# A decoder step with 32 experts: passes of 32 tokens on four column tiles in place of 64 on two

## What is computed

```
top_v, top_i = lax.top_k(h @ r_w + r_b, 4);  top_w = softmax(top_v)      # 4 of 32 experts per token
for e in range(32):
    gu   = h @ w_gu[e] + b_gu[e]                                         # 1024 -> 2048
    gate = min(gu[:, :1024], 7);  up = clip(gu[:, 1024:], -7, 7)
    act  = (up + 1) * gate * sigmoid(1.702 * gate)
    out += combine[:, e] * (act @ w_dn[e] + b_dn[e])                     # 1024 -> 1024
```

```
25 34 47 33 31 60 29 48 24 29 36 25 46 47 42 48 28 36 30 73 44 39 57 19 21 37 29 40 35 79 71 38
```

## Time and profile before

| what | value |
|---|---|
| runs, us | 1500.16, 1504.97, 1509.39; median 1504.97 |
| span of the profiled execution, us | 1507.8 (it has no time of its own beside the span; 2.8 above the median, within the runs) |
| PE busy | 1460.0 us, 97% |
| DVE, ACT busy | 441.6 us, 29%; 197.3 us, 13% |
| moved | 470.78 MB, mean 312 GB/s |
| first expert product, last one | 461.1 us, 1485.7 us |

### The profile page before, as it was taken

The page is one execution under the profiler, slowest core; times in us unless marked ns, Lnnn a source line. Parts: engine busy times, 40 slices in busy tenths (PEclk is TensorE's granted clock), DMA queues, the critical chain, the costliest instruction groups (busy, mean ns, idle before and its releaser), DMA issues.

```text
span 1507.8 us, 18412 instructions
## 1 busy us (share of the span) xinstructions
PE 1460.0 (97%) x6676; PEld 654.1 (43%) x6677; DVE 441.6 (29%) x1096; ACT 197.3 (13%) x334; POOL 21.3 (1%) x35
## 2 busy tenths in 40 slices
PE   5999999999979999999999999999999999999996
PEld 2655566666754333333333333333333333333333
DVE  3133332323373223222322322232232223223226
ACT  2120013000021101111110110111011111111102
POOL 0000000000000000000000000000000000000000
PEclk9999999878998999999999999999999999999998
DMA  9877351104325999999999999997999999996380
GB/s 390 314 286 294 113 181 63 74 12 135 131 112 223 375 417 418 418 417 417 419 418 417 417 419 419 416 417 316 360 418 419 416 418 419 419 416 261 129 332 35
DMA packets 87366, 470.78 MB, mean 312 GB/s; under 512 B 7936, under 2 KB 7952, under 8 KB 51280
## 3 DMA queue, kind: packets, MB, share of 16 engines
q1 hardware_dynamic: 84416, 460.68, 75.5%
q0 software_dynamic: 2352, 7.75, 1.9%
q10 hardware_dynamic: 576, 2.04, 0.3%
HBM read 465.59 MB, written 4.85 MB: 312 GB/s over the span
## 4 chain that ended last, share of the span: by engine, by line
PE 84%; DMA 8%; SPq 5%; DVE 2%; issue 1%; ACT 0%; DVEq 0%
PE bank L866 25%; PE bank L900 14%; PE bank L581 12%; DMA ring<-in_exp_w_gu 7%; PE bank L797 6%; PE bank L778 6%; SPq L434 5%; PE bank L713 3%; PE bank L728 2%; PE bank L579 2%; PE bank L884 1%; PE bank L891 1%; PE bank L664 1%; PE bank L785 1%; PE bank L644 1%; DMA ring<-in_ada_w 1%
## 5 line engine op out<-in xcount | busy, mean ns | idle before, releaser
L866 PE MATMUL bank<-ring,big 128*64 128x512 f32 x2240 | 490.4, 593 | 6.9 <-DMA ring<-in_exp_w_gu 6.9
L866 PEld LDWEIGHTS bank<-ring,big 128*64 128x64 f32 x2240 | 158.2, 137 | 317.6 <-issue 286.2
L900 PE MATMUL bank<-ring,big 128*64 128x512 f32 x1120 | 257.7, 602 | 0.0
L1516 DVE TENSOR_SCALAR big<-bank 128x512 f32<-128x512 f32 x35 | 24.2, 692 | 685.5 <-PE bank L866 685.5
L581 PE MATMUL bank<-hT,ring 128*128 128x320 f32 (+1 forms) x592 | 177.3, 461 | 4.2 <-DVE hT L1161 3.1
L581 PEld LDWEIGHTS bank<-hT,ring 128*128 128x128 f32 (+1 forms) x592 | 117.5, 201 | 69.4 <-issue 27.8
L900 PEld LDWEIGHTS bank<-ring,big 128*64 128x64 f32 x1120 | 74.6, 137 | 129.7 <-issue 127.3
L1505 DVE TENSOR_TENSOR gates<-gates,bank 128x320 f32<-128x320 f32 x272 | 114.2, 481 | 44.5 <-PE bank L797 44.5
L797 PE MATMUL bank<-big 64*128 64x320 f32 x560 | 114.1, 457 | 2.3 <-DVE xT L1559 1.6
L778 PE MATMUL bank<-vtok,big 128*64 128x512 f32 x432 | 100.8, 602 | 0.3 <-DVE big L1446 0.3
L797 PEld LDWEIGHTS bank<-big 64*128 64x128 f32 x560 | 64.0, 185 | 51.5 <-issue 34.9
(11 more groups left out here) (273 smaller groups left out, 846.7 us busy)
## 6 DMA issues: line engine op xcount, KB each, us to landing
ring<-in_exp_w_gu SPq DMA_DIRECT2D x256, 1024.0 KB, 18.1
ring<-in_exp_w_dn SPq DMA_DIRECT2D x128, 1024.0 KB, 16.1
ring<-in_ada_w SPq DMA_DIRECT2D x24, 1024.0 KB, 20.6
ring<-in_w_in SPq DMA_DIRECT2D x20, 1024.0 KB, 9.7
ring<-in_w_out SPq DMA_DIRECT2D x4, 1024.0 KB, 8.5
ring<-in_w_in SPq DMA_DIRECT2D x4, 528.0 KB, 10.4
S<-in_state_hgrn POOLq DMA_DIRECT2D x4, 512.0 KB, 7.5
out_hgrn_sample<-S POOLq DMA_DIRECT2D x4, 512.0 KB, 3.8
```

The lines of the kernel that those rows point to most:

```text
L866: ins = mm(banks[1 + m][64 * h:64 * h + 64, :], h2g[:, half(k)], ring[:, item_slot(k), c:c + 512], start=False, stop=(k == DC - 1))
L900: ins = mm(banks[4][64 * h:64 * h + 64, :], actT[:, half(k)], pair(item_slot(DC + k // 2))[:, k % 2, h * 512:(h + 1) * 512], start=(k == 0 ...
```

## The change

CAP becomes 32. An item's 32 tokens are the stationary operand in four column tiles of 32: tile g holds columns 256g to 256g+255 of each half of the output, so one instruction covers 256 gate and 256 up columns (`gu`, one bank), or 256 columns of `w_dn`'s output. All [128 x 512] buffers of an item become [128 x 256]. The scatter reads 32 rows per feature block, in four row tiles.

All items run in one loop. PE's is now a loop over pairs of experts with an inner loop over the items of each (the table holds the first item of each expert, and item tables are built before item 0). The output biases go through the scatter of item 0, from `dng`, into a `yacc` that is set to zero first. SP's rule stays: buffer s of an expert waits for the last item of the expert before. `NAHEAD` is 0, so the branch that would give some buffers a second home (`late`) is not taken; `late` only gathers tiles of the first stages at one address.

```diff
-CAP = 64
+CAP = 32
+NAHEAD = 0
+GRP = P // CAP
+HALF = D // GRP
...
-        SCATTER = [3, 5, 4, 6, 7, 0, 6, 7]
+        SCATTER = [4, 5, 6, 7, 4, 5, 6, 7]
+        FEATURES = [2 * (n % GRP) + n // GRP for n in range(DC)]
...  SP
-            def expert(e, i):
+            def expert(e, odd, last1, last2):
...
                     elif s == 7:
-                        sp.wait_ge(up_ready, i + 1)
+                        sp.wait_ge(gu_ready, used + 1)
                     elif s == 11:
-                        sp.wait_ge(dn_ready, i + 1)
+                        sp.wait_ge(dn_ready, used + 1)
                     else:
-                        sp.wait_ge(slot_used, i * 10 + (USED0 + (s if s < 7 else s - 1) + 1))
+                        sp.wait_ge(slot_used, used * 10 + (USED0 + (s if s < 7 else s - 1) + 1))
...
-            with sp.Fori(1, E) as e:
-                expert(e, sp.value_load(itemtab[0:1, ds(e + NI, 1)], min_val=0, max_val=NI - 1))
+            expert(1, True, last_item(0), None)
+            with sp.Fori(1, E // 2) as pairs:
+                e = pairs * 2
+                expert(e, False, last_item(e - 1), last_item(e - 2))
+                expert(e + 1, True, last_item(e), last_item(e - 1))
...  PE, one item
-                for m in range(2):
-                    for h in range(2):
-                        mm(banks[1 + m][64 * h:64 * h + 64, :], bsel[0:96, :], bgu[0:96, m * D + h * 512:m * D + (h + 1) * 512],
-                           start=True, stop=False)
+                for g in range(GRP):
+                    mm(out[part(g), :, :], bsel[0:96, :], bias[0:96, :, columns(g)], start=True, stop=False,
+                       tile_position=(0, CAP * g))
                 for k in range(DC):
...
+                    w = item_buffer(k, odd).rearrange("p (m c) -> p m c", m=2)
+                    for g in range(GRP):
+                        last = mm(out[part(g), :, :], h2g[:, chunk(k)], w[:, :, columns(g)], start=False, stop=(k == DC - 1),
+                                  tile_position=(0, CAP * g))
+                    last.then_inc(gu_ready if k == DC - 1 else slot_used, 1)
                 gather(i + 1)
+                pe.wait_ge(dn_copied, i + 1)
+                pe.wait_ge(selw_copied, i + 1)
+                pe.wait_ge(summed, i * 8 + 1)
+                scatter(i, range(GRP))
                 pe.wait_ge(act_ready, i + 1)
...              two transposes of the activation
+                flip_gathered(i + 1)
+                scatter(i, range(GRP, 2 * GRP))
                 pe.wait_ge(act_copied, i + 1)
                 for k in range(DC):
...
+                    for g in range(GRP):
+                        last = mm(banks[2][part(g), HALF:2 * HALF], actT[:, chunk(k)],
+                                  pair(item_slot(DC + k // 2))[:, k % 2, columns(g)],
+                                  start=(k == 0), stop=(k == DC - 1), tile_position=(0, CAP * g))
+                    if k % 2:
+                        last.then_inc(dn_ready if k == DC - 1 else slot_used, 1)
+                flip_weights(i + 1)
...  scatter
+                    x, g = n // GRP, n % GRP
+                    if n >= GRP:
+                        pe.wait_ge(summed, i * 8 + (n - GRP + 2))
+                    mm(banks[SCATTER[n]][:, 0:T], dng[part(g), x * P:(x + 1) * P], SelWT[part(g), :],
+                       start=True, stop=True, tile_position=(CAP * g, 0)).then_inc(scattered, 1)
...  PE's loops
+            with pe.Fori(0, E // 2) as pairs:
+                e = pairs * 2
+                n0, n1, n2 = first_item(e), first_item(e + 1), first_item(e + 2)
+                with pe.Fori(n0, n1) as i:
+                    item(i, pairs, False)
+                with pe.Fori(n1, n2) as i:
+                    item(i, pairs, True)
...  DVE, before item 0
+            nc.vector.memset(yacc[:, :, :], 0.0).then_inc(summed, 1)
```

More of the change, by code:

```diff
@@ L41 @@
 NI = E + MAXEXTRA + 1
+NTHR = -(-T // CAP)
 EPS = 1e-6
@@ L256, in build @@
         SelWT = take(T)
-        gtok = take(512)
-        h2g = take(DC * CAP)
-        gbuf, ubuf, sbuf_, actb, actT, dng = (take(512) for _ in range(6))
+        gtok, h2g = take(HALF), take(HALF)
+        gbuf, ubuf, sbuf_, actb, actT, dng = (take(HALF) for _ in range(6))
+        off[0] = 2 * HT + 2048
         bgu = take(1024).bitcast(BF16)
-        bsel = take(32).bitcast(BF16)
+        bdn = take(HALF)
+        bsel = take(CAP // 2).bitcast(BF16)
         posI = take(3 * NI).rearrange("p (a i) -> p a i", a=3)
@@ L264, in build @@
         OHI = take(NI)
+        ohi_from = take(NI)
         yacc = gates
@@ L279, in build @@
         ngt = rtake(1)
[L280 to L283, removed]
+        over = rtake(NTHR, 1)
+        nitems, bounds = rtake(1, 1), rtake(2, 1)
         posT = small[0:E, 0:T]
-        combT = small[0:E, T:2 * T]
-        logT = combT
-        thrrep = rtake(P, 1)
+        logT = small[0:E, T:2 * T]
+        startrep = rtake(P, 1)
         frow = rtake(NI, 1)
@@ L364, in item_landed_count, with item_buffer @@
             return 16 * ((NPRE + s) // NSLOT + 1)
+        def item_buffer(s, odd):
+            return late[:, s * SLOT:(s + 1) * SLOT] if odd and s < NAHEAD else ring[:, item_slot(s), :]
         def pair(n):
@@ L761, in _, with chunk, part, columns @@
             last.then_inc(turn_filled, 1)
-            for bank in (0, 1, 2):
+            for bank in (0, 1, 2, 3):
                 wait_taken(pe, [n for n in range(TURN["count"]) if TURNS[n][2] == bank][-1])
-            wait_taken(pe, TURN["tok21"])
-            def half(k):
-                at = (k % 4) * P + (k // 4) * CAP
+            def chunk(k):
+                at = (k % 2) * P + (k // 2) * CAP
                 return slice(at, at + CAP)
+            def part(g):
+                return slice(CAP * g, CAP * g + CAP)
+            def columns(g):
+                return slice(HALF * g, HALF * g + HALF)
             def gather(j):
@@ new lines, in _ @@
+            for s in range(3):
+                last = mm(b[0:E, 0:1], sel[:, s, :], ones[:, 0:1], start=(s == 0), stop=(s == 2))
+            last.then_inc(turn_filled, 1)
+            wait_taken(pe, TURN["tok21"])
+            gather(0)
+            pe.wait_ge(nitems_ready, 1)
+            b = open_turn("place")
+            mm(b[0:96, 0:1], C("before96", E), nitems[0:E, 0, :], start=True, stop=True)
+            mm(b[0:96, 1:2], C("upto96", E), nitems[0:E, 0, :], start=True, stop=True)
+            mm(b[0:1, 2:2 + E], nitems[0:E, 0, :], C("before96", E)[:, 0:E], start=True, stop=True)
@@ new lines, in _ @@
+            mm(b[0:1, 2 + E:3 + E], nitems[0:E, 0, :], ones[0:E, 0:1], start=True, stop=True).then_inc(turn_filled, 1)
+            flip_gathered(0)
+            pe.wait_ge(comb_ready, 1)
+            b = open_turn("posT")
+            for p, (t0, tn) in enumerate(TILES):
+                last = nc.tensor.transpose(b[0:E, t0:t0 + tn], posm[0:tn, p, :], ident[0:tn, 0:tn])
+            last.then_inc(turn_filled, 1)
+            flip_weights(0)
+            pe.wait_ge(ohi_ready, 1)
+            b = open_turn("xitems")
@@ L923, in _ @@
+            count = first_item(E)
+            pe.wait_ge(dn_copied, count + 1)
+            pe.wait_ge(selw_copied, count + 1)
+            pe.wait_ge(summed, count * 8 + 1)
             pe.wait_ge(h2g_copied, count + 1)
-            scatter(count - 1, range(8))
+            scatter(count, range(8))
             for n in range(8):
                 pe.wait_ge(x3sq_ready, n + 1)
-                last = mm(banks[1][:, 0:T], ones[:, :], hT[:, 4 * (n % 2) + n // 2, :], start=(n == 0), stop=(n == 7))
+                last = mm(banks[1][:, 0:T], ones[:, :], hT[:, FEATURES[n], :], start=(n == 0), stop=(n == 7))
```

338 lines of the change are left out of this document (128 added, 210 removed).

## The result

The changed kernel took 1604.4 us in the median of four runs (1599.0 to 1607.6), the kernel before 1506.3 (1500.2 to 1509.4, four runs): 1.066 times the time, interval 1.062 to 1.069. It is slower, as forecast, and inside the range, but 47 us under the forecast of 1651 and outside the forecast's own range of 1630 to 1680. The profiled execution took 1597.2 us.

The account below looks back on a forecast made before the run. Transfers bound single-item experts, and the ring's restart adds 6.3 us behind doubles. Start 466.2, experts and end gave 1620; 34 for the clock made 1654 profiled, 1651 as median; range 1602 to 1705, its own 1630 to 1680.

Parts of the forecast that it names:

- the likeliest forecast: SP's ring restarts the transfers behind every expert with two or three items: 1651 us, chance 0.62.
- rival P: From the experiments: PE's chain of items sets the time, the ring is incidental; one item per expert takes 396 us off.
- restart hidden: At SP's wait for buffer 0, the restart costs nothing: 1491 us, not slower; chance 0.04.
- tiles in series: On PE, the four column tiles run one after another: over 2200 us in all; chance 0.02.
- The gap: Between experts' first issues, a double takes 36.4 us, 6.3 more than the 30.1 of a single.
- The item: PE's time for one item: 6.9 + 5.7 + 3.5 + 1.3 = 17.4 us.
- G: End of the last `w_gu` chunk; `w_dn` starts 5.7 us after it, with DVE's sums setting the stretch.
- The start: Before the experts: tables before item 0 and clearing `yacc` cost 3 us, so expert 1's first issue comes at 466.2.
- The clock: PE at 1.2 GHz in `w_dn` and the stretch before it, behind singles and elsewhere: 34 us on top.
- clock stays at 2.4 GHz: Rival: PE's clock doesn't fall in the item: 1617 us, chance 0.17.

Follow-up runs that it names:

- the same edit: On the changed kernel, DVE adds the scatter's eight products before forming the one-hots and bias selector: 1599.7 us; together with second homes for three buffers, 1520.7 us.
- one: Changed kernel with one item per expert, tokens past the 32nd left out: 1426.6 us, 0.948 times the kernel before.
- min2: Changed kernel with at least two items per expert, the second empty for up to 32 tokens: 1675.9 us, 1.113 times the kernel before.

## Why the prediction was right, and where it was off

- **The mechanism.** The kernel is 98 us slower, where the forecast had 146. The case of the likeliest forecast, the restart behind every expert of two or three items, is what happened. It was shown in four ways: by the trace (stretches without traffic, issues 35.5 and 52.0 apart), by taking it away in two steps, by adding it to the singles, and by removing it whole in the kernel with one item each (together with the items, for which rival P would have taken off 396 us and 178 went). The rivals "restart hidden" (1491) and "tiles in series" are out; `w_gu` at 6.9 us shows the four tiles side by side.
- **The gap**, 6.3 forecast, 5.4 found. From the issue at 898.98 the last group of `w_dn` starts 32.6 later (32.8 forecast), and the next expert's issue comes 3.0 behind that, not 3.6. The 1.3 for flips, switching, biases and the loop was 0.8 here, and the first chunk and the issue took what was forecast. Over 17 doubles and three triples (52.0, not 53.8) this is 17 us of the 57. The end of that double's first item, from which its second starts at once:

```profile
927.56 2.80 PE L867 MATMUL bank<-ring,big 128*32 128x256 f32 x48
931.54 1.07 PE L867 MATMUL bank<-ring,big 128*32 128x256 f32 x16 [1.18 <-DMA ring<-in_exp_w_dn]
932.54 0.64 PE L824 MATMUL bank<-consts,big 128*128 128x128 f32 x3
933.11 0.40 PE L842 MATMUL bank<-big 96*32 96x512 bf16 x4
```

- **The item**, 17.4 forecast, 16.5 found without the turn of the loop and 17.8 with it; G was 5.2, not 5.7. It counts in the triples and at the end alone.
- **The start**: expert 1's first issue came at 461.4, not 466.2 (5 us). The tables cost about what was taken or more, with 3.5 us of idle before the first L842, but the stages ahead of them ended 6 us earlier (their last product began at 421.7, before at 427.8), with a granted clock of 0.94 between 120 and 240 us where it was 0.90. That part is no effect of the change to the experts.
- **The clock, the step that failed.** I priced it at 34 us; it cost next to nothing. That is what the sum below leaves for it, and the rows say why. It did fall where I said, behind a single, where eight products per buffer are paced by the transfers:

```profile
673.83 1.07 PE L848 MATMUL bank<-ring,big 128*32 128x512 f32 x8 [1.42 <-DMA ring<-in_exp_w_gu]
...
681.29 1.93 PE L848 MATMUL bank<-ring,big 128*32 128x512 f32 x8 [0.55 <-DMA ring<-in_exp_w_gu]
...
688.74 1.83 PE L848 MATMUL bank<-ring,big 128*32 128x512 f32 x8 [0.55 <-DMA ring<-in_exp_w_gu]
690.39 1.47 PE L802 MATMUL bank<-vtok,big 128*32 128x256 f32 x24
```

```profile
681.00:686.00 5.00, 3.87 (x16) 0.40 (x16) 0.00 (x0) 0.00 (x0) 0.00 (x0) 0.50 1.01 421
...
690.00:695.00 5.00, 4.52 (x47) 2.33 (x40) 4.29 (x13) 1.46 (x4) 0.00 (x0) 0.97 1.02 409
```

  At 1.2 GHz (granted 0.50) a group takes 1.93 us and still waits 0.55 for the next buffer. The clock was back before L802, and the stretch to `w_dn` ran at 2.4 GHz. The working had put the fall on the stretch and on `w_dn`, where a double can't hide it; the trace of before could have said that a chunk at the low clock (twice 0.86, under 2 us) is shorter than a buffer (2.5 us). `w_dn` ran at the low clock for its whole length four times (5.35 us, not 3.66): in item 0 and in the last items of experts 12, 20 and 30 (at 474.50, 874.26, 1164.45 and 1536.48). The item behind each of them still waits 0.4 to 0.7 us for its own last buffer, so the 1.7 us are hidden there too. The Trainium skill (TensorE: Matmul & The Clock Gate, "HAM oscillation") tells of short bursts between transfers that run at the low clock; these rows agree, at five buffers of eight. Of the cases on record, "clock stays at 2.4 GHz" (1617) had the right price and the wrong picture.
- **The luck in it.** The measured 1604.4 lies 2 us above the low end of the range. Two terms, the clock and the gap, were too high by 34 and 17 us, both the same way; the range held them because it took in the clock at full speed and a shorter stretch G.

In sum, for the profiled execution: 1654 forecast, less 5 for the start, 17 for gap and triples, 1 at the end, 34 for the clock, is 1597.

## What to carry to other kernels

When a ring holds exactly one group of weights and a buffer is given back by the *last* pass over it, the number of passes decides whether the transfers stop; a faster pass can't repair that, and buffers that open the next group early can. Price a low clock only where nothing else ends later than the slowed work: it was free beside the restart, and not free once TensorE set the pace. Before shortening an item, check that the item is the bound: the same edit was worth 5 us here and 23 with the restart gone.

## What the runs showed of the hardware

- Four column tiles of 32 in float32 run side by side: 64 products of 512 columns in 6.87 us (107 ns each), a fourth of the 0.43 us that an untiled product of 512 columns takes in the same kernel (32 of them in 13.9 us from 77.14 on), and 64 of 256 columns in 3.6 us (56 ns).
- A queue that has stood still lands its first MB 4.7 to 4.9 us after the issue, where one in flow lands a buffer every 2.5.
- A turn of TensorE's outer loop stood on the engine for 1.2 us with three register loads and for 0.7 with one, and for 2.2 and 1.7 where three transposes no longer stood right before it. Behind stops of 2.2 us the clock was low in the next `w_gu` in 8 and 10 of 15 cases, behind stops of 1.7 in 4 and 1.
- The lower clock alone says nothing of the time: the kernel with the lowest mean (0.835, `one`, which leaves tokens out) was the fastest, and the one at 0.965 (`min2`) the slowest of those tried.
